# The attention mask written into the score banks by ScalarE instead of added by TensorE

## The chip, the cores and the metric

One core of a Trainium2 chip runs the whole program in one launch. The metric is the device time of that core in microseconds (us); lower is better. All times here come from three timed runs of the kernel before and from one profiled execution of it.

## The reference, cut to what matters

The program is a model of 13 phases over 256 tokens (272 with 16 meta tokens in the first half): eight feed-forward networks, two "hybrid mixers" with stick-breaking attention beside a 31-tap convolution, one differential attention, one retention, and one norm. The change touches the two mixers. Their attention is:

```python
z = jnp.einsum('bhqd,bhkd->bhqk', qb, kh) * scale
valid = key_pos < qpos
log_keep = jnp.where(valid, jax.nn.log_sigmoid(-z), 0.0)
after = lax.cumsum(log_keep, axis=3, reverse=True) - log_keep
attn = jnp.where(valid, jnp.exp(jax.nn.log_sigmoid(z) + after), 0.0)
return jnp.einsum('bhqk,bhkd->bhqd', attn, vh)
```

There are 8 heads of 64 dimensions. Only keys before the query count; the others are masked by adding -1e30 to z. The feed-forward networks, `(silu(x @ w_gate) * (x @ w_up)) @ w_down`, matter here because their buffers move in memory.

## The kernel before, in words

All matrices are float32. Every weight panel (128 x 1024 or 128 x 1408) is loaded by SyncE's queue into `raw`, split by ScalarE into a rounded part `whi` (L432) and by VectorE into the rest `wlo` (L439), and used once: TensorE forms three products per tile, x_hi by whi (L416), x_lo by whi (L423) and x_hi by wlo (L424). The ring of panels has four slots. Each matmul has its own weight load (PEld in the profile), which overlaps the matmul before it.

**Order of the work.** There is no scheduler: each engine's list is written out by hand, and waits on semaphores join them. In a mixer TensorE runs panels 0 to 16, and then four groups p = 0 to 3, one per pair of heads. A group is: `scores(p)` (18 small matmuls L720 into banks 6 and 7, and two matmuls L727 that add the mask, identity by `mask_r`, to columns 0:144 and 288:432 of each bank), a panel, `weighted_values(2p-1)` (L770), a panel, `suffix_sums(2p)` (L751 to L756), a panel, `suffix_sums(2p+1)` and `weighted_values(2p)`, a panel. In group 3 a matmul L795 with `mean_512` stands behind `suffix_sums(6)`; it waits for `ysum_step`, the sum over the convolution's channels that GpSimd makes (L2153, L2158) when its taps (L2149) are through.

ScalarE's list in a group: `log_terms` of both heads (L1262 to L1266, behind `z_full`), `terms_hi` (L1273), two panels' splits, `weights_hi(2p)` (L1279 and L1282, exponentials of the bank), four tap products for GpSimd (L1217), a panel's split, `weights_hi(2p+1)`, `out_hi(2p)` (L1287), up to four tap products, a panel's split. `weights_hi` is the last reader of its bank before the next pair's scores, which wait for it through `at_hi_ready`.

**Where the buffers lie.** The program's buffers stand in each partition one behind the other, in the order of their declaration, each rounded up to 32 bytes. `raw`, `whi`, `wlo`, `h` and `u` come before `consts`; `hid` (the input of the feed-forwards' second product), `qk`, `ao_hi`, `ao_lo`, `ry`, `dy_hi`, `rqk_hi` and others come behind it. `consts` has 10 x 128 floats (5120 bytes). From the sizes follows the offset of the moving operand x of a matmul against the weight tile that is loaded while it runs, in bytes modulo 256:

| operands | matmuls | offset before |
|---|---|---|
| u by whi, wlo | all gate, up and mixer input panels | 192 |
| hid by whi, wlo | 8 feed-forwards, second product: 2640 of 256 columns, 1584 of 272 | 192 |
| ry by whi, wlo | output of the retention: 384 of 256 columns | 192 |
| dy_hi, dy_lo by dw | three panels of the differential attention | 64 |
| qk, ao by whi, wlo | tail of the mixers | 192, 192, and 128 for the third of each three (x and weights both advance by 64 bytes per tile, so the next tile's weights are 64 nearer) |
| rqk_hi, rqk_lo by each other | retention scores | 0 |

For hid: 22528 (whi) + 22528 (wlo) + 8704 (h) + 20480 (u) + 3 x 1088 + 32 + 5120 (consts) + 3712 (constants and gains) + 96 (the place in `hid`) = 86464 = 337 x 256 + 192.

Of the kernel before, what the change touches and what calls it, by code (L numbers as in the profile page):

```python
# [12 lines left out]
T = META + SEQ  # L13
# [149 lines left out]
def build(nc, w8, w11, xT, small, cst, lam, outT):  # L163
# [7 lines left out]
    with ctx:  # L171
        def sb(name, shape, dt=f32, where=None):
            return (where or ctx).enter_context(nc.sbuf_tensor(name, shape, dt))

        def sem(name):
            return ctx.enter_context(nc.semaphore(name))
# [14 lines left out]

        consts = sb("consts", [128, CONSTS, 128])
        mean_d, mean_512, mean_128, mean_64, ident, ones_f, tri_f = (consts[:, i, :] for i in range(7))
        masks = consts[:, :, :].rearrange("p a c -> p (a c)")[:, 7 * 128:7 * 128 + 2 * MASKED]
        ones_r = sb("ones_r", [128, 128], f32r)
        tri_r = sb("tri_r", [128, 128], f32r)
        ident_r = sb("ident_r", [128, 128], f32r)
# [83 lines left out]
        with ExitStack() as area:  # L283
# [60 lines left out]

        qk_hi_ready, qk_ready, vt_full, v_hi_ready, v_ready = (
            sem(s) for s in ("qk_hi_ready", "qk_ready", "vt_full", "v_hi_ready", "v_ready"))
        z_full, az_done, e_done, l_done, nlk_done = (
            sem(s) for s in ("z_full", "az_done", "e_done", "l_done", "nlk_done"))
        lk_hi_ready, lk_ready, c_full = (sem(s) for s in ("lk_hi_ready", "lk_ready", "c_full"))
# [284 lines left out]
        def _(pe):  # L634
# [55 lines left out]
            def mix(y, l):  # L690
# [15 lines left out]
                def scores(p):  # L706


                    pe.wait_ge(qk_ready, 8 * l + 2 * p + 2)
                    if p == 0:  # L710
                        pe.wait_ge(const_r, 5 + l)
                        pe.wait_ge(v_ready, 3 * l + 2)
                    if PAIRS * l + p > 0:
                        pe.wait_ge(at_hi_ready, SB_HEADS * l + 2 * p)
                    for i, (s0, c0, w) in enumerate(S_TILES):
                        for n, (kt, qt) in enumerate(((0, 8), (0, 12), (4, 8))):
                            ks, qs = (kt + p) * T + KEY_AT[i], (qt + p) * T + s0
                            for m in range(2):
                                rows = slice(64 * m, 64 * m + 64)
                                pe.matmul(bank[6 + m][:, c0:c0 + w], flat[rows, ks:ks + 128], flat[rows, qs:qs + w],  # L720
                                          start=(i == 0 and n == 0), stop=False, skip_group_check=True)


                    for m in range(2):
                        whole = bank[6 + m][:, :]
                        two = bass.AP(whole.tensor, whole.offset, [whole.ap[0], [SECOND, 2], [1, MASKED]])
                        pe.matmul(two, ident_r[:, :], mask_r[:, :].rearrange("p (a c) -> p a c", c=MASKED), start=False,  # L727
                                  stop=True, skip_group_check=True).then_inc(z_full, 1)
# [403 lines left out]
        def _(act):  # L1132
# [66 lines left out]
            def mix(y, l):  # L1199
# [75 lines left out]
                def weights_hi(hd):  # L1275
                    act.wait_ge(c_full, H + hd + 1)
                    if hd >= 1:
                        act.wait_ge(at_ready, H + hd)
                    act.activation(ex[:, :], bank[6 + hd % 2][:, 0:SW], ACT.Exp)  # L1279
                    if hd >= 2:  # L1280
                        act.wait_ge(o_full, H + hd - 1)
                    act.activation(at_hi[:, hd % 2, :], bank[6 + hd % 2][:, 0:SW], ACT.Exp).then_inc(at_hi_ready, 1)  # L1282

                def out_hi(hd):
                    rows = slice(64 * (hd % 2), 64 * (hd % 2) + 64)
                    act.wait_ge(o_full, H + hd + 1)
                    act.activation(ao_hi[rows, hd // 2, :], bank[5][rows, 0:T], ACT.Copy).then_inc(ao_hi_ready, 1)  # L1287

                for p in range(PAIRS):
                    j, n = FIRST_PANELS + 4 * p, POOL_HEAD_TAPS[p]  # L1290
                    log_terms(2 * p)
                    tap_products(n[0])
                    log_terms(2 * p + 1)
                    terms_hi(2 * p)
                    panel(j)
                    terms_hi(2 * p + 1)
                    if p > 0:
                        out_hi(2 * p - 1)
                    panel(j + 1)
                    weights_hi(2 * p)  # L1300
                    tap_products(n[1])
                    if p == PAIRS - 1:
                        for c in range(CH):
                            act.wait_ge(yc_done, CH * l + c + 1)
                            act.activation(cpad[:, c, CPAD:CPAD + N2], proj[:, A_SLOT + c, W2], ACT.Square)\
                               .then_inc(ysq_done, 1)
                    panel(j + 2)
                    if p == PAIRS - 1:
                        weights_hi(2 * p + 1)
                        out_hi(2 * p)  # L1310
                    if p < PAIRS - 1:
                        weights_hi(2 * p + 1)
                        out_hi(2 * p)
                    tap_products(n[2])
                    panel(j + 3)
                j = FIRST_PANELS + 4 * PAIRS
# [260 lines left out]
        def _(dve):  # L1577
# [95 lines left out]
            def mix(y, l):  # L1673
# [33 lines left out]
                if l == 0:  # L1707
# [6 lines left out]
                    dve.tensor_copy(tri_r[:, :], tri_f).then_inc(const_r, 1)  # L1714
                    dve.tensor_copy(ident_r[:, :], ident).then_inc(const_r, 1)
                    dve.tensor_copy(mean_64r[:, :], mean_64).then_inc(const_r, 1)
                dve.tensor_copy(mask_r[:, :], masks).then_inc(const_r, 1)
                def qk_lo(i):
                    hi, lo = (i // 2, 4 + i // 2) if i % 2 else (8 + i // 2, 12 + i // 2)
                    dve.wait_ge(qk_hi_ready, 8 * l + i + 1)  # L1720
# [389 lines left out]
        @block.gpsimd  # L2110
        def _(pool):
            pool_update(pool, 0)
            pool.dma_start(consts[:, 1:CONSTS, :], cst[:, 128:CONSTS * 128].rearrange("p (a c) -> p a c", c=128))\
                .then_inc(const_loaded, 16)
            pool.dma_start(sgain[:, :], small[:, GAINS:GAINS + SMALLS]).then_inc(const_loaded, 16)
            pool.dma_start(lam_in[:, :, :], lam.partition_broadcast(128)).then_inc(const_loaded, 16)
# [1 line left out]
            for y, kind in enumerate(PHASES):  # L2118
                if kind in ("da", "rt"):

                    pool.wait_ge(panel_used, BASE[y]["P"])
                    at = {"da": CONSTS * 128, "rt": CONSTS * 128 + 384}[kind]
                    dst = {"da": dist, "rt": rdist}[kind]
                    pool.dma_start(dst[:, :], cst[:, at:at + 384]).then_inc(table_loaded, 16)
                if kind == "da":
# [54 lines left out]
GAINS = len(PHASES) * KD  # L2180
SMALLS = 2 * CH * (CONV_K + 3) + 3 + 16
CONST_LOADS = 3
CONSTS = 10


def tables():

    p = np.arange(128)[:, None]
    c = np.arange(128)[None, :]
    one = np.ones((128, 128))  # L2190
    parts = [one / D, one / 512, one / 128, (p // 64 == c // 64) / 64.0, p == c, -one, -1.0 * (p >= c)]
    far = 1e30
    last = np.where((p >= 128 - (T - 256)) & (c > p - (128 - (T - 256))), 0.0, -far)[:, 0:T - 256]
    seen = np.zeros((128, 3 * 128 - 2 * MASKED + T - 256))
    parts += [last, np.where(c > p, 0.0, -far), np.where(c > p, 0.0, -far), seen]
    for d in (p - c, 128 + p - np.arange(256)[None, :],
              np.arange(256)[None, :] - p, c - p):
        parts.append(np.where(d >= 0, d, far))
    return np.ascontiguousarray(np.concatenate([np.asarray(x, np.float64) for x in parts], 1), np.float32)
# [79 lines left out]
```

## Time and profile before

| | us |
|---|---|
| median of 3 runs (2171.69 to 2171.99) | 2171.73 |
| the profiled execution's own time | 2172.23 |
| its span | 2170.4 |
| TensorE matmuls busy | 2159.0 (99%) |
| VectorE busy | 1473.0 (68%) |
| ScalarE busy | 1202.2 (55%) |
| GpSimd busy | 283.9 (13%) |

The mean granted TensorE clock of the execution is 1.000, that is 2.4 GHz. A matmul's duration in a row is its latency through a pipeline: consecutive matmuls start much closer together (some 0.12 us) than they last (some 0.28 us). What a stream costs is read from the distance of the starts.

### The profile page before, as it was taken

The page shows a single profiled execution, that of the slowest core. Times are in us where ns is not written, and L with a number is a line of the kernel's source. Part 1 is how long each engine was busy: PE and PEld are TensorE (multiplying, and loading weights), DVE is VectorE, ACT ScalarE, POOL GpSimd, SP SyncE. Part 2 cuts the span into 40 slices and gives each one's busy share as a digit, 9 for nine tenths or more (in the row PEclk, how much of TensorE's full clock was granted, in tenths as well). Part 3 has the DMA queues.
Part 4 walks back from the last instruction along what each step waited for, and adds up shares of the span by engine and source line. Part 5 has one row for each costly group of instructions (what it writes and reads, how often), then busy time and mean ns, then how long its engine had stood idle before and what let it go on. Part 6 is the DMA issues. An engine that isn't in the chain of part 4 may idle for free.

```text
span 2170.4 us, 48317 instructions
## 1 busy us (share of the span) xinstructions
PE 2159.0 (99%) x18139; PEld 2141.7 (99%) x18139; DVE 1473.0 (68%) x2242; ACT 1202.2 (55%) x1752; POOL 283.9 (13%) x328
## 2 busy tenths in 40 slices
PE   8999999999999999999999999999999999999999
PEld 8999999999999999999999999999999999999999
DVE  6655998665566579876657657976656745686663
ACT  6444786544444368755555546865445535565552
POOL 0001661100100136220020011010010010101000
PEclk9999999999999999999999999999999999999999
DMA  6555435556455554455656655356656655445664
GB/s 233 176 192 167 163 118 175 175 174 198 153 181 186 182 165 142 149 177 193 205 180 194 200 188 170 117 184 191 207 173 195 209 178 180 161 158 195 193 217 131
DMA packets 100401, 386.57 MB, mean 178 GB/s; under 512 B 11312, under 2 KB 12464, under 8 KB 100304
## 3 DMA queue, kind: packets, MB, share of 16 engines
q1 hardware_dynamic: 99648, 383.89, 53.7%
q0 software_dynamic: 368, 1.26, 0.2%
q8 instruction: 62, 1.02, 0.2%
q14 instruction: 35, 0.29, 0.0%
q10 hardware_dynamic: 288, 0.12, 0.0%
HBM read 384.18 MB, written 1.05 MB: 177 GB/s over the span
## 4 chain that ended last, share of the span: by engine, by line
PE 91%; DVE 6%; ACT 2%; issue 1%; DMA 0%; SPq 0%; ACTq 0%; DVEq 0%
PE bank L423 28%; PE bank L416 28%; PE bank L424 28%; DVE wlo L439 2%; DVE bank L1702 1%; PE bank L1056 1%; PE bank L1058 1%; PE bank L1057 1%; ACT whi L432 1%; PE bank L1103 0%; PE bank L770 0%; DVE proj L1688 0%; PE bank L947 0%; PE bank L950 0%; PE bank L949 0%
## 5 line engine op out<-in xcount | busy, mean ns | idle before, releaser
L416 PE MATMUL bank<-u,whi 128*128 128x256 f32 (+2 forms) x3776 | 1062.6, 281 | 7.3 <-DVE u L477 7.3
L423 PE MATMUL bank<-u,whi 128*128 128x256 f32 (+1 forms) x3776 | 1062.1, 281 | 0.0
L424 PE MATMUL bank<-u,wlo 128*128 128x256 f32 (+1 forms) x3776 | 1060.0, 281 | 0.0
L439 DVE TENSOR_TENSOR wlo<-raw,whi 128x1024 fp32r<-128x1024 f32 (+1 forms) x677 | 892.7, 1321 | 186.1 <-ACT whi L432 185.5
L432 ACT ACTIVATE whi<-raw 128x1024 fp32r<-128x1024 f32 (+1 forms) x677 | 743.5, 1112 | 192.3 <-PE bank L424 172.0
L416 PEld LDWEIGHTS bank<-u,whi 128*128 128x128 f32 x3776 | 711.3, 188 | 8.5 <-DVE wlo L439 7.2
L423 PEld LDWEIGHTS bank<-u,whi 128*128 128x128 f32 x3776 | 711.3, 188 | 0.9 <-issue 0.2
L424 PEld LDWEIGHTS bank<-u,wlo 128*128 128x128 f32 x3776 | 711.1, 188 | 0.0
L416 PE MATMUL bank<-hid,whi 128*128 128x256 f32 (+1 forms) x1408 | 394.2, 280 | 0.0
L423 PE MATMUL bank<-hid,whi 128*128 128x256 f32 (+1 forms) x1408 | 394.2, 280 | 0.0
L424 PE MATMUL bank<-hid,wlo 128*128 128x256 f32 (+1 forms) x1408 | 394.2, 280 | 0.0
L1639 DVE TENSOR_TENSOR up<-bank,R 128x256 f32<-128x256 f32 (+1 forms) x176 | 75.8, 431 | 289.5 <-PE bank L424 289.5
L416 PEld LDWEIGHTS bank<-hid,whi 128*128 128x128 f32 x1408 | 264.6, 188 | 0.0
L424 PEld LDWEIGHTS bank<-hid,wlo 128*128 128x128 f32 x1408 | 264.6, 188 | 0.0
L423 PEld LDWEIGHTS bank<-hid,whi 128*128 128x128 f32 x1408 | 264.6, 188 | 0.0
L464 ACT ACTIVATE u<-h,gain 128x256 fp32r<-128x256 f32 (+1 forms) x88 | 44.2, 512 | 268.3 <-DVE h L1604 262.5
L1174 ACT ACTIVATE sl<-gt 128x256 f32<-128x256 f32 (+1 forms) x160 | 67.7, 423 | 198.0 <-DVE gt L1637 198.0
L1179 ACT ACTIVATE hid<-pr 128x256 f32 (+2 forms) x160 | 67.8, 424 | 152.9 <-DVE pr L1644 152.9
L1604 DVE SCALAR_TENSOR_TENSOR h<-bank,h 128x256 f32<-128x256 f32 (+1 forms) x88 | 37.9, 430 | 163.9 <-PE bank L424 163.8
L513 POOL TENSOR_TENSOR ssq<-h 128x256 f32<-128x256 f32 (+1 forms) x10 | 6.2, 624 | 1029.0 <-DVE h L1604 1029.0
L2149 POOL TENSOR_TENSOR proj<-proj,tprod 128x272 f32<-128x272 f32 (+1 forms) x120 | 121.7, 1034 | 54.6 <-ACT tprod L1217 49.8
L518 POOL TENSOR_TENSOR sq<-h 128x256 f32<-128x256 f32 (+1 forms) x70 | 45.0, 644 | 345.9 <-DVE h L1604 344.9
(297 smaller groups left out, 2190.8 us busy)
## 6 DMA issues: line engine op xcount, KB each, us to landing
raw<-w SPq DMA_DIRECT2D x552, 512.0 KB, 3.3
raw<-w SPq DMA_DIRECT2D x128, 704.0 KB, 4.8
h<-xT SPq DMA_DIRECT2D x4, 272.0 KB, 5.6
outT<-h SPq DMA_DIRECT2D x8, 128.0 KB, 5.0
consts<-cst POOLq DMA_DIRECT2D x1, 576.0 KB, 5.0
dist<-cst POOLq DMA_DIRECT2D x1, 192.0 KB, 2.8
rdist<-cst POOLq DMA_DIRECT2D x1, 192.0 KB, 3.7
sgain<-small POOLq DMA_DIRECT2D x1, 145.5 KB, 5.4
```

What stands on the lines that cost most here:

```text
L416: pe.matmul(out[:, cut:cols], w, x[:, cut:cols], start=first, stop=False, skip_group_check=True)
L423: pe.matmul(out, w_h, x_lo, start=False, stop=False, skip_group_check=True)
L424: return pe.matmul(out, w_l, x_hi, start=False, stop=last, skip_group_check=True)
L432: act.activation(weights(0, n), raw[:, n % RING, 0:COLS[n]].rearrange("p (k c) -> p k c", c=128), ACT.Copy).then_inc(hi_ready, 1)
L439: dve.tensor_tensor(weights(1, n), raw[:, n % RING, 0:COLS[n]].rearrange("p (k c) -> p k c", c=128), weights(0, n), ALU.subtract).then_inc ...
L464: act.activation(u_at(y, 0, f), h[:, f, win(y)], ACT.Copy, scale=norm_gain(y, f)).then_inc(u_hi_ready, 1)
L518: pool.tensor_tensor(sq[:, win(y)], h[:, f, win(y)], h[:, f, win(y)], ALU.mult).then_inc(sq_done, 1)
L1174: act.activation(sl[:, p, W], gt[:, p, W], ACT.Silu).then_inc(silu_done, 1)
L1179: act.activation(hid_at(y, 0, f), pr[:, p, W], ACT.Copy).then_inc(hid_hi_ready, 1)
L1604: dve.scalar_tensor_tensor(out=h[:, f, W], in0=src, scalar=factor, in1=h[:, f, W], op0=ALU.mult, op1=ALU.add).then_inc(h_done, 1)
L1639: dve.tensor_tensor(up[:, p, W], bank[(g + 1) % 4][:, 0:N], R[:, W], ALU.mult).then_inc(a_evac, 1)
L2149: pool.tensor_tensor(acc, acc, tprod[:, m % TAP_RING, W2], ALU.add)\
```

## The change

ScalarE's new step `masked(hd)` copies the mask of all 432 score columns from `consts` (float32, the middle 144 columns zero) into bank 6 or 7. It stands behind `weights_hi(2p)` for head 2p+2 and behind `out_hi(2p)` for head 2p+3, for p = 0 to 2. The scores of pairs 1 to 3 then start no new sum (start is set only at p = 0), so that they are added to what lies in the bank; they wait for the new semaphore `z_masked`, and their last matmul on each bank gives `z_full`. The two mask matmuls stay for pair 0 of each mixer. `consts` becomes 7 x 128 + 432 = 1328 floats in place of 1280, one flat row, loaded by the same DMA in one piece per partition; `mask_r` is cast from its first and third 144 columns.

```diff
-        consts = sb("consts", [128, CONSTS, 128])
-        mean_d, mean_512, mean_128, mean_64, ident, ones_f, tri_f = (consts[:, i, :] for i in range(7))
-        masks = consts[:, :, :].rearrange("p a c -> p (a c)")[:, 7 * 128:7 * 128 + 2 * MASKED]
+        consts = sb("consts", [128, CONSTS])
+        mean_d, mean_512, mean_128, mean_64, ident, ones_f, tri_f = (consts[:, 128 * i:128 * i + 128] for i in range(7))
+
+        mask = consts[:, CONSTS - SW:CONSTS]
+        masks = mask.rearrange("p (a c) -> p a c", c=MASKED)[:, 0:3:2, :]
...
+                    if p > 0:
+                        pe.wait_ge(z_masked, (SB_HEADS - 2) * l + 2 * p)
...
-                                pe.matmul(bank[6 + m][:, c0:c0 + w], flat[rows, ks:ks + 128], flat[rows, qs:qs + w],
-                                          start=(i == 0 and n == 0), stop=False, skip_group_check=True)
-
-
-                    for m in range(2):
+                                mm = pe.matmul(bank[6 + m][:, c0:c0 + w], flat[rows, ks:ks + 128], flat[rows, qs:qs + w],
+                                               start=(p == 0 and i == 0 and n == 0), stop=False, skip_group_check=True)
+                                if p > 0 and i == 2 and n == 2:
+                                    mm.then_inc(z_full, 1)
+
+                    for m in range(2 if p == 0 else 0):
...
+                def masked(hd):
+
+                    act.wait_ge(at_hi_ready, H + hd - 1)
+                    act.activation(bank[6 + hd % 2][:, 0:SW], mask, ACT.Copy).then_inc(z_masked, 1)
+
...
                     weights_hi(2 * p)
+                    if p < PAIRS - 1:
+                        masked(2 * p + 2)
                     tap_products(n[1])
...
                         weights_hi(2 * p + 1)
                         out_hi(2 * p)
+                        masked(2 * p + 3)
                     tap_products(n[2])
...
-CONSTS = 10
+CONSTS = 7 * 128 + SW
```

**What moves in memory.** Everything behind `consts` lies 192 bytes further on; `whi`, `wlo` and `u` stay. The offsets of the table become: hid and ry by whi and wlo 128 (86464 + 192 = 338 x 256 + 128), qk and ao 128, 128 and 64; u stays at 192; pairs that both lie behind `consts` (dy by dw, rqk by rqk) keep theirs.

**What moves on the engines.** TensorE in the second mixer at the scores of pair 2, in the program before (`qk` are the scores, `u` by `whi` the next panel):

```order
L424 MATMUL bank<-u,wlo 128x256
L720 MATMUL bank<-qk 128x272 [waits at_hi_ready,qk_ready]
L720 MATMUL bank<-qk 128x272 x5
L720 MATMUL bank<-qk 128x144 x6
L720 MATMUL bank<-qk 128x16 x6
L727 MATMUL bank<-mask_r,ident_r 128x2x144 x2
L416 MATMUL bank<-u,whi 128x256 [waits a_evac,lo_ready]
```

The same place in the changed program (L725 is the score's line there, L419, L426 and L427 the products'):

```order
L427 MATMUL bank<-u,wlo 128x256
L725 MATMUL bank<-qk 128x272 [waits z_masked,at_hi_ready,qk_ready]
L725 MATMUL bank<-qk 128x272 x5
L725 MATMUL bank<-qk 128x144 x6
L725 MATMUL bank<-qk 128x16 x6
L419 MATMUL bank<-u,whi 128x256 [waits a_evac,lo_ready]
```

The two mask matmuls are gone in three groups of each mixer, and the first score has one more wait.

ScalarE in the second mixer, second half of group 2, before:

```order
L1279 ACTIVATE ex<-bank 128x432 [waits at_ready,c_full]
L1282 ACTIVATE at_hi<-bank 128x432 [waits o_full]
L1217 ACTIVATE tprod<-cpad,sgain 128x256 [waits pool_tap_done] x4
L432 ACTIVATE whi<-raw 128x1024 [waits panel_used,raw_loaded3]
L1279 ACTIVATE ex<-bank 128x432 [waits at_ready,c_full]
L1282 ACTIVATE at_hi<-bank 128x432 [waits o_full]
L1287 ACTIVATE ao_hi<-bank 64x272 [waits o_full]
L1217 ACTIVATE tprod<-cpad,sgain 128x256 [waits pool_tap_done] x4
```

And in the changed program (L1293 is the new copy):

```order
L1285 ACTIVATE ex<-bank 128x432 [waits at_ready,c_full]
L1288 ACTIVATE at_hi<-bank 128x432 [waits o_full]
L1293 ACTIVATE bank<-consts 128x432 [waits at_hi_ready]
L1223 ACTIVATE tprod<-cpad,sgain 128x256 [waits pool_tap_done] x4
L435 ACTIVATE whi<-raw 128x1024 [waits panel_used,raw_loaded3]
L1285 ACTIVATE ex<-bank 128x432 [waits at_ready,c_full]
L1288 ACTIVATE at_hi<-bank 128x432 [waits o_full]
L1298 ACTIVATE ao_hi<-bank 64x272 [waits o_full]
L1293 ACTIVATE bank<-consts 128x432 [waits at_hi_ready]
L1223 ACTIVATE tprod<-cpad,sgain 128x256 [waits pool_tap_done] x4
```

Both copies stand ahead of tap products for GpSimd; the second has only these between it and the next panel's split.

## Rows read from the trace of the kernel before

**Rows 1.** The page, busy time of the engines
```profile
PE 2159.0 (99%) x18139; PEld 2141.7 (99%) x18139; DVE 1473.0 (68%) x2242; ACT 1202.2 (55%) x1752; POOL 283.9 (13%) x328
```

**Rows 2.** The page, the chain that ended last, by engine
```profile
PE 91%; DVE 6%; ACT 2%; issue 1%; DMA 0%; SPq 0%; ACTq 0%; DVEq 0%
```

**Rows 3.** Waits of TensorE: for whom, us in total, times, longest
```profile
PE bank L416 <- DVE u L477: 7.3, 1, 7.3
```

**Rows 4.** Timeline of TensorE, first mixer: start us, us
```profile
275.73 0.52 PE L727 MATMUL bank<-mask_r,ident_r 128*128 128x288 f32 x2
276.09 0.29 PE L416 MATMUL bank<-u,whi 128*128 128x272 f32 x1
276.22 0.28 PE L423 MATMUL bank<-u,whi 128*128 128x272 f32 x1
...
280.02 0.37 PE L416 MATMUL bank<-u,whi 128*128 128x272 f32 x1
280.23 0.29 PE L423 MATMUL bank<-u,whi 128*128 128x272 f32 x1
```

**Rows 5.** ScalarE's operation of 432 columns from SBUF to SBUF: busy us, mean ns
```profile
L1273 ACT ACTIVATE lk_hi<-proj 128x432 fp32r<-128x432 f32 x16 | 8.9, 556 | 1.8 <-DVE proj L1752 1.8
```

**Rows 6.** Timeline of ScalarE and TensorE, end of group 0, first mixer
```profile
272.44 0.39 ACT L1287 ACTIVATE ao_hi<-bank 64x272 fp32r<-64x272 f32 x1
274.58 1.22 PE L720 MATMUL bank<-qk 64*128 64x272 f32 x18
```

**Rows 7.** Timeline of ScalarE, second mixer, group 2
```profile
871.41 0.53 ACT L1282 ACTIVATE at_hi<-bank 128x432 fp32r<-128x432 f32 x1
871.82 1.70 ACT L1217 ACTIVATE tprod<-cpad,sgain 128x256 f32<-128x256 f32 x4
```

**Rows 8.** Timeline of GpSimd, then TensorE, first mixer, then second mixer
```profile
315.25 2.08 POOL L2158 TENSOR_TENSOR sq<-sq,proj 128x272 f32<-128x272 f32 x2
...
318.61 0.48 PE L795 MATMUL bank<-sq,consts 128*128 128x272 f32 x1
...
872.41 10.96 POOL L2149 TENSOR_TENSOR proj<-proj,tprod 128x256 f32<-128x256 f32 x9 [4.90 <-ACT tprod L1217]
884.33 2.08 POOL L2158 TENSOR_TENSOR sq<-sq,proj 128x256 f32<-128x256 f32 x2
...
886.71 0.46 PE L795 MATMUL bank<-sq,consts 128*128 128x256 f32 x1
```

**Rows 9.** Timeline of TensorE, a feed-forward's second product, then the second mixer's tail
```profile
1099.92 0.28 PE L424 MATMUL bank<-hid,wlo 128*128 128x256 f32 x1
...
1101.39 0.28 PE L416 MATMUL bank<-hid,whi 128*128 128x256 f32 x1
...
934.80 0.28 PE L423 MATMUL bank<-qk,whi 128*128 128x256 f32 x1
...
936.34 0.28 PE L424 MATMUL bank<-qk,wlo 128*128 128x256 f32 x1
```

**Rows 10.** TensorE's matmuls by operands and shape: count, busy us, mean ns
```profile
L423 PE MATMUL bank<-hid,whi 128*128 128x256 f32 x880 | 242.9, 276 | 0.0
L423 PE MATMUL bank<-hid,whi 128*128 128x272 f32 x528 | 151.3, 286 | 0.0
L423 PE MATMUL bank<-ry,whi 128*128 128x256 f32 x128 | 35.3, 276 | 0.0
L1036 PE MATMUL bank<-dy_hi,dw_hi 128*128 128x256 f32 x24 | 6.6, 276 | 0.0
L424 PE MATMUL bank<-qk,wlo 128*128 128x256 f32 x96 | 27.1, 283 | 0.0
L416 PE MATMUL bank<-qk,whi 128*128 128x272 f32 x96 | 27.7, 289 | 0.0
L423 PE MATMUL bank<-qk,whi 128*128 128x272 f32 x96 | 27.4, 285 | 0.0
L1089 PE MATMUL bank<-rqk_lo,rqk_hi 128*128 128x256 f32 x8 | 2.2, 280 | 0.0
```

More of the change, by code:

```diff
@@ L346, in build @@
             sem(s) for s in ("qk_hi_ready", "qk_ready", "vt_full", "v_hi_ready", "v_ready"))
+        z_masked = sem("z_masked")
         z_full, az_done, e_done, l_done, nlk_done = (
@@ L1716, in mix @@
                     dve.tensor_copy(mean_64r[:, :], mean_64).then_inc(const_r, 1)
-                dve.tensor_copy(mask_r[:, :], masks).then_inc(const_r, 1)
+                dve.tensor_copy(mask_r[:, :].rearrange("p (a c) -> p a c", c=MASKED), masks).then_inc(const_r, 1)
                 def qk_lo(i):
@@ L2112, in _ @@
             pool_update(pool, 0)
-            pool.dma_start(consts[:, 1:CONSTS, :], cst[:, 128:CONSTS * 128].rearrange("p (a c) -> p a c", c=128))\
+            pool.dma_start(consts[:, 128:CONSTS], cst[:, 128:CONSTS])\
                 .then_inc(const_loaded, 16)
@@ L2121, in _ @@
                     pool.wait_ge(panel_used, BASE[y]["P"])
-                    at = {"da": CONSTS * 128, "rt": CONSTS * 128 + 384}[kind]
+                    at = {"da": CONSTS, "rt": CONSTS + 384}[kind]
                     dst = {"da": dist, "rt": rdist}[kind]
@@ L2193, in tables @@
     last = np.where((p >= 128 - (T - 256)) & (c > p - (128 - (T - 256))), 0.0, -far)[:, 0:T - 256]
-    seen = np.zeros((128, 3 * 128 - 2 * MASKED + T - 256))
-    parts += [last, np.where(c > p, 0.0, -far), np.where(c > p, 0.0, -far), seen]
+    parts += [last, np.where(c > p, 0.0, -far), np.zeros((128, MASKED)), np.where(c > p, 0.0, -far),
+              np.zeros((128, T - 256))]
     for d in (p - c, 128 + p - np.arange(256)[None, :],
```

## The prediction

> **What bounds the kernel now.** I read the page's busy times first: TensorE's matmuls are busy for 2159.0 of 2170.4 us [rows 1]. The chain that ended last then shows that this is the bound, not merely activity: 91% of it is TensorE [rows 2], and the longest of TensorE's waits in total is 7.3 us, a single one at the start of the program [rows 3]. So the time is the number of matmuls times the distance of their starts. An edit pays if it removes matmuls or shortens that distance, and costs if it lengthens it; what ScalarE, VectorE or GpSimd do counts only where they make TensorE wait. The timeline gives the distances and the grouping by shape the durations, which serve as a second gauge: a longer distance shows in both.
>
> The sum is made against the profiled execution, 2172.23 us (2170.4 of span and 1.8 around it). The median of the runs is 2171.73, 0.5 less, and I take 0.5 off at the end.
>
> **Part 1: the mask matmuls that go.** Six groups lose a pair of L727. From the first of the pair to the panel's first L416 it is 276.09 - 275.73 = 0.36 us [rows 4]. Not all of it comes back. Behind the pair, L416 follows L423 at 276.22 - 276.09 = 0.13; where L416 stands directly behind a small matmul, the same step takes 280.23 - 280.02 = 0.21 [rows 4], and that is where it will stand now. So a group gives 0.36 - 0.08 = 0.28 us, and six give -1.7. Bounds: nothing of the step is lost, 6 x 0.36 = -2.2; the whole 0.21 is new, 6 x 0.15 = -0.9.
>
> **Part 2: ScalarE's twelve copies.** No row shows ScalarE writing 432 columns from SBUF into a bank. From SBUF to SBUF such an operation takes 0.56 us [rows 5], from a bank 0.53 [rows 7]; I take 0.53. The nearest other rows of one pass over a tile bound it, 0.38 (L1287, 272 columns [rows 6]) and 0.56; the second rival has a higher price. The copies are 6.4 us of ScalarE, which is busy 55%; the question is who waits.
>
> (a) The scores wait for `z_masked`. The tightest place is group 0 of the first mixer: `out_hi` ends at 272.44 + 0.39 = 272.83 and the scores start at 274.58 [rows 6], 1.75 us later. The first copy delays everything behind it by about 0.57: 0.41 of issue distance plus the 0.12 for which the copy must wait until its own predecessor has ended (871.41 + 0.53 against the 871.82 at which the next operation starts now [rows 7]), and a little for the semaphore. The second adds 0.53. That is 1.1 of 1.75; 0.65 is left, so I cost it at nothing. Queued behind the copies are tap products and the split of a panel that TensorE needs only three panels later (24 matmuls of 0.12 each, almost 9 us), so the split's delay is hidden too.
>
> (b) The tap products feed GpSimd. In group 2 of the second mixer GpSimd starts nine adds right behind the delayed product, at 872.41, runs them back to back, and ends its sums at 884.33 + 2.08 = 886.41; TensorE's L795, which waits for them, starts at 886.71 [rows 8]. The slack is 0.30 us. TensorE will be there 3 x 0.28 = 0.84 earlier. GpSimd's start moves by +0.57 (the copy) and -0.56 (two groups shortened ahead of it), so not at all. TensorE then waits 0.84 - 0.30 = 0.5 us. Bounds: 0 (if the product comes as early as TensorE does) and +1.1 (the full 0.57 on top). In the first mixer the same slack is 318.61 - (315.25 + 2.08) = 1.28 us [rows 8], more than 0.84, and I take nothing.
>
> **Part 3: the 192 bytes.** This edit is not about the mask, and it is the largest term. `consts` grows by 48 floats, so `hid` and `ry` move against `whi` and `wlo`: their offset goes from 192 to 128 modulo 256, at every one of their matmuls. The rows show two speeds for one and the same shape of 256 columns. In the stream of `hid`, 13 steps take 1101.39 - 1099.92 = 1.47 us, 113 ns each; in the mixer's tail 13 steps take 936.34 - 934.80 = 1.54, 118.5 each [rows 9]. The durations say the same: 276 ns for hid and ry (offset 192) and dy by dw (64), 283 for the matmul of qk that meets 128, and 280 for rqk, at 0 [rows 10]. The pattern that fits is that a weight load and a moving operand whose addresses differ by a multiple of 128 disturb each other. It is a reading of few rows, and qk and rqk differ from hid in more than this.
>
> The price: between ends far apart, nothing and the 7 ns of qk by wlo (283 against 276), I take the row in which every step lies on a multiple of 128, as it will in hid: rqk, 280 against 276, 4 ns. 3 x 880 of hid and 3 x 128 of ry are 3024 matmuls x 4 = 12.1 us. For 272 columns the difference is smaller: 289 and 285 for qk, in the middle 287, against 286 for hid, 1 ns x 1584 (3 x 528) = 1.6 [rows 10]. Together +13.7. Bounds: 0, and 3024 x 7 + 1584 x 3 = 25.9. Below nothing: no row of 256 columns is faster than 276, whatever its offset, so I leave only a small chance for a gain. qk and ao go from one multiple of 128 in three to two in three; their speed is off already, and I take 0.
>
> A rule of the Trainium skill speaks against this term. TensorE: Matmul & The Clock Gate, section "Step-by-step: what each phase is for", says that the array has two independent read ports, and that loading the next weights does not take bandwidth from the running matmul. By it part 3 would be 0 and the time that of the first rival below; the trace agrees as far as loads overlap matmuls everywhere, but it does not explain two speeds for one shape.
>
> **The rest.** The cast of the mask reads the same number of columns, the load of `consts` is one DMA at the start, needed only in the first mixer: 0.
>
> **Sum.** 2172.23 - 1.7 + 0.5 + 13.7 = 2184.7; less 0.5 for the median, 2184.2, say 2184.
>
> **Rivals.**
> First, not slower: addresses do not matter and only the queues count. The offset's term is 0, and -1.7 + 0.5 = -1.2 on the median gives 2170.5. For it: hid has no row at 128, and qk's slower step could come from its other layout (tiles 1088 bytes apart). Against it: rqk, of another layout, is slow too, and rows at 64 and 192 are alike. The mechanism decides at 0 ns per step; up to 1.8 ns (5.5 us over 3024) the time would still be called the same.
>
> Second, the wait moves to ScalarE: the copy into a bank takes twice what I take, 1.1 us, so that both copies delay `out_hi`'s successor by 2.2 and the scores wait some 0.5 us in each of six groups. Without the address term that is -1.2 + 3.0 = +1.8, 2173.5. Rows 5 and 7 speak against it: operations of 432 columns take 0.53 to 0.56.
>
> Third, the change does more than it says in the good direction: at 128 the load and the operand interleave better than at 192, for example 3 ns per matmul, 3024 x 3 = -9, with the -1.2 giving 2161.5. No row supports it.
>
> **How the numbers follow.** Forecast (address term between 1.8 and 8 ns) 0.59; first rival 0.33; second 0.03; third 0.05. About 0.2% (4.3 us) is what a measurement of this kernel can tell from no change. Slower by more: 0.59. Within: 0.33 + 0.03 = 0.36. Faster: 0.05. The range must take in the first rival: it goes from 2169.5 (part 1 at its bound of -2.2 and no wait in 2b) to 2194 (the address term at 23.5, near its upper end). The forecast's own range is 2178 to 2194.
>
> **What would show it.** hid and ry by whi and wlo of 256 columns at 280 ns or more, with starts 117 to 120 ns apart, while u stays at 276 and 113: part 3 right. If they stay at 276, the step of part 3 has failed, and the time is near 2170.5. Twelve rows of the copy at 0.5 to 0.56 us and no wait of the scores on them: part 2a right. A wait of L795 on GpSimd of about 0.5 us in the second mixer: part 2b right. Scores followed by L416 and L423 at a distance of 0.21 us: part 1 right. If u too changes speed, the cause is not the offset that I name.

## The result and the profile after

| | before | after |
|---|---|---|
| median of 5 runs each, same chip, us | 2171.99 (2171.69 to 2172.32) | 2194.85 (2194.60 to 2198.95) |
| profiled execution and its span, us | 2172.23, 2170.4 | 2194.60, 2192.8 |

By the medians the changed kernel is slower by 22.9 us. Over all runs it takes 1.0111 of the time before, interval 1.0101 to 1.0122; two of its five runs lie some 4 us above the other three. The forecast was slower by 12, with 2194 as the end of its range. The direction is right; the largest term was put at 13.7 us and measured 21.6.

The page's busy times and its chain by engine, in the changed kernel [rows 1, 2]:

```profile
PE 2180.7 (99%) x18127; PEld 2163.4 (99%) x18127; DVE 1470.8 (67%) x2242; ACT 1206.6 (55%) x1764; POOL 283.5 (13%) x328
...
PE 92%; DVE 3%; issue 2%; ACT 2%; POOL 1%; DMA 0%; POOLq 0%; ACTq 0%; DVEq 0%
```

There are 12 matmuls fewer (18127 against 18139), and TensorE is busy for 21.7 us more. The span grew by 22.4. TensorE's waits are no place for that [rows 3]; the columns are the total in us, how often, and the longest:

```profile
PE bank L419 <- DVE u L480: 7.3, 1, 7.3
PE bank L801 <- POOL sq L2172: 0.8, 1, 0.8
PE bank L744 <- DVE proj L1702: 0.4, 1, 0.4
PE bank L757 <- DVE lk_lo L1773: 0.4, 1, 0.4
```

The first is the start of the program, as before. The second and the fourth are new and small: the sums' matmul L801 waits for GpSimd, and a suffix sum L757 for `lk_lo`. A wait of 0.2 on VectorE at the tail of the second mixer is new too, and stands in the kernel with the 192 bytes alone as well. The scores (L725) do not appear.

Which matmuls slowed is read from the grouping by operands and shape [rows 5, 10], count, busy us, mean ns:

```profile
L426 PE MATMUL bank<-u,whi 128*128 128x256 f32 x2272 | 630.5, 278 | 0.0
L419 PE MATMUL bank<-hid,whi 128*128 128x256 f32 x880 | 247.7, 281 | 0.0
L419 PE MATMUL bank<-hid,whi 128*128 128x272 f32 x528 | 153.0, 290 | 0.0
L426 PE MATMUL bank<-ry,whi 128*128 128x256 f32 x128 | 36.3, 284 | 0.0
L427 PE MATMUL bank<-qk,wlo 128*128 128x256 f32 x96 | 26.7, 278 | 0.0
L1293 ACT ACTIVATE bank<-consts 128x432 f32<-128x432 f32 x12 | 6.3, 529 | 0.2
```

`hid` went from 276 to 281 ns and from 286 to 290; `ry` from 276 to 284; `u`, whose place did not change, is at 278 (277 before). The starts say how much of that is time. A feed-forward's second product after [rows 9], start and duration in us; 13 steps lie between the two rows, and 1.54 us, 118.5 ns each where it was 113:

```profile
1109.92 0.28 PE L427 MATMUL bank<-hid,wlo 128*128 128x256 f32 x1
...
1111.46 0.28 PE L419 MATMUL bank<-hid,whi 128*128 128x256 f32 x1
```

Over a whole stretch, from the first start of a second product to its last, the traces give the following (each stretch of hid has 527 steps, that of ry 383):

| stretch | count | before, us | after, us | difference in all |
|---|---|---|---|---|
| hid, 256 columns | 5 | 59.73 | 62.54 | +14.1 |
| hid, 272 columns | 3 | 65.00 | 66.75 | +5.3 |
| ry, 256 columns | 1 | 43.75 | 46.00 | +2.3 |

That is 21.6 of the span's 22.4. From the last second product ahead of it to the first panel of the next feed-forward, the first mixer is 0.16 us longer than before (its tail's matmuls of `qk`, 272 columns, take 0.22 more) and the second 0.81 shorter. So some 1.4 us lie elsewhere. The largest part is in the retention: it has five short stretches of u by `whi` and `wlo`, and four of them run at 118 ns a step where it was one before, which makes 0.95 us in all. The offset of u is 192 in both kernels. By shape, 1819.5 to 1826 us in the kernel before, then 1835.5 to 1842 in the changed one:

```profile
L424 PE MATMUL bank<-u,wlo 128*128 128x256 f32 x20 | 5.5, 276 | 0.0
...
L427 PE MATMUL bank<-u,wlo 128*128 128x256 f32 x20 | 5.6, 281 | 0.0
```

The experiments come back to such a change of speed without a change of offset.

The removed matmuls, in group 0 of the first mixer after [rows 4, 6]; `x18` are the scores in one row:

```profile
275.78 1.21 PE L725 MATMUL bank<-qk 64*128 64x272 f32 x18
276.92 0.39 PE L419 MATMUL bank<-u,whi 128*128 128x272 f32 x1
277.15 0.28 PE L426 MATMUL bank<-u,whi 128*128 128x272 f32 x1
277.27 0.29 PE L427 MATMUL bank<-u,wlo 128*128 128x272 f32 x1
```

L426 follows L419 at 0.23 us, where 0.21 was foreseen. From the first score to the third product it is 277.27 - 275.78 = 1.49 us; over the six groups the mean of that distance fell from 1.75 to 1.49, which is 0.26 per group and 1.6 us in all. ScalarE at the same place:

```profile
274.24 0.38 ACT L1298 ACTIVATE ao_hi<-bank 64x272 fp32r<-64x272 f32 x1
274.52 0.52 ACT L1293 ACTIVATE bank<-consts 128x432 f32<-128x432 f32 x1
```

The copy ends at 275.04, and the scores that need it start at 275.78: a slack of 0.74 us, where 0.65 was foreseen. In the second mixer GpSimd, then TensorE [rows 8]:

```profile
877.43 10.43 POOL L2163 TENSOR_TENSOR proj<-proj,tprod 128x256 f32<-128x256 f32 x9 [5.09 <-ACT tprod L1223]
...
888.82 2.84 POOL L2172 TENSOR_TENSOR sq<-sq,proj 128x256 f32<-128x256 f32 x2
...
891.71 0.70 PE L801 MATMUL bank<-sq,consts 128*128 128x256 f32 x2 [0.77 <-POOL sq L2172]
```

The nine adds moved with the program and take 10.43 us, where they took 10.96. The two sums behind them take 2.84 us, where they took 2.08; L801 waits 0.77 for them. One by one, with what VectorE does beside them, the sums are, first in the kernel before, then in the changed one:

```profile
884.33 0.75 POOL L2158 TENSOR_TENSOR sq<-sq,proj 128x256 f32<-128x256 f32 x1
885.20 0.60 DVE L1759 TENSOR_TENSOR lk_lo<-proj,lk_hi 128x432 fp32r<-128x432 f32 x1
885.22 1.19 POOL L2158 TENSOR_TENSOR sq<-sq,proj 128x256 f32<-128x256 f32 x1
```

```profile
888.79 0.60 DVE L1773 TENSOR_TENSOR lk_lo<-proj,lk_hi 128x432 fp32r<-128x432 f32 x1
888.82 1.17 POOL L2172 TENSOR_TENSOR sq<-sq,proj 128x256 f32<-128x256 f32 x1
889.64 1.43 DVE L442 TENSOR_TENSOR wlo<-raw,whi 128x1024 fp32r<-128x1024 f32 x1
890.13 1.52 POOL L2172 TENSOR_TENSOR sq<-sq,proj 128x256 f32<-128x256 f32 x1
```

A sum takes 1.17 to 1.19 us beside `lk_lo`, 1.52 beside the rest of a split into `wlo`, and 0.75 where neither runs. In the kernel before one of the two sums met such an operation of VectorE, in the changed one both did.

### The profile page after: what moved, and what is told of

Its sections match the earlier page's. It is cut to its first block, busy times and chain, and to the rows that moved or that the text cites. A ratio compares the mean times of both kernels' runs of the same rounds, so it can differ in the third digit from the quotient of the medians.

```text
span 2192.8 us, 48305 instructions
## 1 busy us (share of the span) xinstructions
PE 2180.7 (99%) x18127; PEld 2163.4 (99%) x18127; DVE 1470.8 (67%) x2242; ACT 1206.6 (55%) x1764; POOL 283.5 (13%) x328
## 4 chain that ended last, share of the span: by engine, by line
PE 92%; DVE 3%; issue 2%; ACT 2%; POOL 1%; DMA 0%; POOLq 0%; ACTq 0%; DVEq 0%
PE bank L426 28%; PE bank L419 28%; PE bank L427 28%; DVE wlo L442 1%; POOL proj L2163 1%; DVE bank L1716 1%; PE bank L1062 1%; PE bank L1064 1%; PE bank L1063 1%; ACT whi L435 1%; PE bank L889 1%; PE bank L1109 0%; PE bank L776 0%; PE bank L953 0%; PE bank L955 0%
## 5 line engine op out<-in xcount | busy, mean ns | idle before, releaser
L419 PE MATMUL bank<-u,whi 128*128 128x256 f32 (+2 forms) x3776 | 1063.4, 282 | 7.3 <-DVE u L480 7.3
L426 PE MATMUL bank<-u,whi 128*128 128x256 f32 (+1 forms) x3776 | 1062.2, 281 | 0.0
L427 PE MATMUL bank<-u,wlo 128*128 128x256 f32 (+1 forms) x3776 | 1060.2, 281 | 0.0
L419 PEld LDWEIGHTS bank<-u,whi 128*128 128x128 f32 x3776 | 711.3, 188 | 8.8 <-DVE wlo L442 7.5
L426 PEld LDWEIGHTS bank<-u,whi 128*128 128x128 f32 x3776 | 710.9, 188 | 0.9 <-issue 0.2
L427 PEld LDWEIGHTS bank<-u,wlo 128*128 128x128 f32 x3776 | 710.8, 188 | 0.0
L419 PE MATMUL bank<-hid,whi 128*128 128x256 f32 (+1 forms) x1408 | 400.6, 285 | 0.0
L427 PE MATMUL bank<-hid,wlo 128*128 128x256 f32 (+1 forms) x1408 | 400.6, 285 | 0.0
L426 PE MATMUL bank<-hid,whi 128*128 128x256 f32 (+1 forms) x1408 | 400.6, 285 | 0.0
L427 PEld LDWEIGHTS bank<-hid,wlo 128*128 128x128 f32 x1408 | 265.1, 188 | 0.0
L419 PEld LDWEIGHTS bank<-hid,whi 128*128 128x128 f32 x1408 | 265.1, 188 | 0.0
L426 PEld LDWEIGHTS bank<-hid,whi 128*128 128x128 f32 x1408 | 265.1, 188 | 0.0
```

The source lines that it names most:

```text
L419: pe.matmul(out[:, cut:cols], w, x[:, cut:cols], start=first, stop=False, skip_group_check=True)
L426: pe.matmul(out, w_h, x_lo, start=False, stop=False, skip_group_check=True)
L427: return pe.matmul(out, w_l, x_hi, start=False, stop=last, skip_group_check=True)
```

## The experiments

Each kernel is the one before or the changed one with the lines shown. "Stretch" is the distance from first to last start as in the table above; the offsets are of the moving operand against `whi` and `wlo`, modulo 256 bytes.

**Is it the 192 bytes, or the mask?** `e2_shift_only` is the kernel before with the bytes alone; `e1_mask_realigned` is the changed kernel with 64 bytes more, so that everything behind `consts` lies 256 bytes further on than before and all offsets are the old ones.

```diff
e2_shift_only, against before
         consts = sb("consts", [128, CONSTS, 128])
...
+        sb("consts_pad", [128, 48])
e1_mask_realigned, against after
         consts = sb("consts", [128, CONSTS])
...
+        sb("consts_pad", [128, 16])
```

> The kernel before, with 48 unused floats behind consts: the change's 192 bytes without its mask part. Address theory: hid 281 and 290 ns, ry 282 to 285, as in the change, and a time of 2172.0 + 22.9 + 0.8 = 2195.7, somewhat above the change. Rival (the rhythm comes from the mask part): the time of before, 2172, and hid at 276.

> The change, with 16 floats (64 bytes) left free behind consts, so that everything behind it lies 256 bytes further on than before and all offsets against whi and wlo are those of before. Address theory: hid by whi of 256 columns back at 276 ns and 113 ns apart (after: 281 and 118.7), of 272 columns at 286 (after: 290), ry at 276; the loss of some 22 us is gone and only the mask part is left, -1.6 for six shorter groups and +0.8 for L801's wait on GpSimd: about 2171.2, 0.8 below before. Rival (the mask matmuls that are gone let TensorE's stream enter another rhythm, which it keeps in the feed-forwards): hid stays at 281 and the time near 2194.

`e2_shift_only`: 2194.76 us (2194.44 to 2195.05), ratio 1.0105 (1.0089 to 1.0120). The 192 bytes alone, without any copy, give the whole loss. `e1_mask_realigned`: median 2176.66 of 11 runs (2171.16 to 2177.77), ratio 1.0013 (1.0004 to 1.0022). The ratio takes in all runs, whose means are 2174.9 and 2172.0: the whole change with the old offsets is slower by 0.13%, and its runs are spread wider than those of the kernel before (the last experiments). By operands and shape, first `e2_shift_only`, then `e1_mask_realigned`:

```profile
L424 PE MATMUL bank<-hid,whi 128*128 128x256 f32 x880 | 247.6, 281 | 0.0
L424 PE MATMUL bank<-hid,whi 128*128 128x272 f32 x528 | 153.0, 290 | 0.0
L424 PE MATMUL bank<-ry,whi 128*128 128x256 f32 x128 | 36.0, 281 | 0.0
```

```profile
L427 PE MATMUL bank<-hid,whi 128*128 128x256 f32 x880 | 242.9, 276 | 0.0
L427 PE MATMUL bank<-hid,whi 128*128 128x272 f32 x528 | 151.3, 286 | 0.0
L427 PE MATMUL bank<-ry,whi 128*128 128x256 f32 x128 | 35.9, 280 | 0.0
```

hid follows the offset exactly, with stretches of 62.54 and 66.75 us in the one and 59.73 and 65.00 in the other. ry does not: it is slow in `e1_mask_realigned` (280 ns, 45.25 us) though its offset is 192 again. That, and the two heaps in which the runs of this kernel lie, is a thing of its own, taken up last.

**Which offsets are bad?** The place of `hid` is set for each feed-forward by a table, in floats, so one execution tries eight places on the kernel before. Apart from 128 and 192, each offset rests on one product of a shape, in one execution.

```diff
-HID_PLACE = {0: (24, 0), 2: (24, 0), 3: (24, 0), 5: (24, 0), 7: (24, 0), 9: (24, 0), 10: (24, 0), 12: (24, 0)}
+HID_PLACE = {0: (40, 0), 2: (56, 0), 3: (8, 0), 5: (8, 0), 7: (40, 0), 9: (56, 0), 10: (16, 0), 12: (32, 0)}   # e3_hid_places
+HID_PLACE = {0: (16, 0), 2: (88, 0), 3: (32, 0), 5: (88, 0), 7: (48, 0), 9: (28, 0), 10: (20, 0), 12: (0, 0)}  # e5_hid_places_2
```

> The kernel before, with the place of hid changed feed-forward by feed-forward, nothing else. Offsets modulo 256 of hid against whi and wlo, in the order of the eight second products: 0, 64, 128 (272 columns), then 128, 0, 64, 160, 224 (256 columns). Theory 'multiples of 128 are bad': 64 as fast as 192 (64.9 us a product of 272 columns from the first to the last start, 59.6 of 256), 0 and 128 alike at 66.6 and 62.4; at 160 and 224, half way, anything between. Rival 'only 192 is good': 64 as slow as 128. Rival 'only the absolute address of hid counts, or what others write': the slow products don't follow this order.

> A second map of places of hid in the kernel before. Offsets modulo 256 in the order of the eight second products: 160, 192 (but 256 bytes further on), 224 for 272 columns; then 192 (256 bytes further on), 32, 208, 176, 96 for 256 columns. In the first map only 192 was fast (65.0 and 59.7 us a product), and 0, 64, 128, 160 and 224 cost 1.1 to 3.5 us. Theory 'the offset modulo 256 decides, and only near 192 is good': both products at 192 + 256 fast, 32 and 96 slow (61.8 to 63.2), and 176 and 208 show how wide the good place is. Rival 'the absolute place decides': 192 + 256 is slow too.

One run each: 2190.15 and 2186.43 us. A place of 24 floats is offset 192; each float more adds 4 bytes, so 88 floats are 256 bytes more and 192 again. The stretches in us:

| offset | 0 | 32 | 64 | 96 | 128 | 160 | 176 | 192 | 192, 256 bytes on | 208 | 224 |
|---|---|---|---|---|---|---|---|---|---|---|---|
| 256 columns | 63.22 | 61.49 | 62.07 | 63.23 | 62.54 | 61.84 | 62.85 | 59.73 | 59.73 | 62.80 | 62.35 |
| 272 columns | 66.05 | | 66.75 | | 66.75 | 65.01 | | 65.00 | 65.00 | | 66.05 |

Rows by shape of single feed-forwards. `e3_hid_places` at 0, then at 64:

```profile
L423 PE MATMUL bank<-hid,whi 128*128 128x256 f32 x176 | 49.8, 283 | 0.0
...
L424 PE MATMUL bank<-hid,wlo 128*128 128x256 f32 x176 | 49.1, 279 | 0.0
```

and `e5_hid_places_2` at 192 and 256 bytes on, then at 32:

```profile
L423 PE MATMUL bank<-hid,whi 128*128 128x256 f32 x176 | 48.6, 276 | 0.0
...
L423 PE MATMUL bank<-hid,whi 128*128 128x256 f32 x176 | 49.2, 279 | 0.0
```

The reading "multiples of 128 disturb" falls: 32, 96, 160, 176, 208 and 224 are slow too. Of the ten offsets tried with 256 columns only 192 ran fast, and it comes again 256 bytes further on; for 272 columns 160 is as good. The place of before was the good one, and the change left it.

For 64 this is not shown. Its stretch of 62.07 us goes in steps of 117 to 119 ns, 117.8 in the mean. At 128 they are uneven, 115 to 122, while 117 to 119 with the same mean, and the same 62.07 us, is what hid at 192 does in the second rhythm found below. So the product at 64 may have been in that rhythm, and no second run of it was made.

**Is it where hid lies, or where it lies against the weights?** `e6_all_shifted` moves everything from `whi` on by 64 bytes, so that no offset changes; `e7_u_too` moves everything behind `wlo` by 192, so that u is at 128 as well; `e8_wlo_only` puts `whi` at the good offset and `wlo` at 128, one load in three.

```diff
e6_all_shifted, behind the declaration of raw
+        sb("w_pad", [128, 16])
e7_u_too, behind the declaration of wlo
+        sb("w_pad", [128, 48])
e8_wlo_only, behind whi and behind wlo
+        sb("w_pad", [128, 16])
...
+        sb("x_pad", [128, 48])
```

> The kernel before with 16 unused floats between raw and whi: all weights and all moving operands lie 64 bytes further on, and no offset between them changes. Offset theory: 2171.8, all products as before. Rival (absolute addresses decide): hid, ry and perhaps u slow, 20 us or more.

> The kernel before with 48 unused floats between wlo and h: u moves by 192 bytes against whi and wlo too, to offset 128, beside hid, ry, qk and ao. Offset theory: what hid lost in e2 (5.35 ns a step at 256 columns, 3.3 at 272) is lost by u as well: 6788 x 5.35 + 4500 x 3.3 = 51 us on top of 23, about 2246. Rival (something of hid and ry alone, for example who writes them while they are read): 2195 as e2.

> The kernel before with 16 unused floats between whi and wlo and 48 between wlo and h: the offset of every moving operand to whi is 192 as before, that to wlo 128. One weight load in three has the bad offset. If each load pays for itself, hid loses a third of what it lost in e2: 59.73 + 0.9 = 60.7 us a product, and all of the kernel about a third of e7's 74: 2196. If one bad load in three keeps the stream in the slow rhythm (as in qk before, 118.4 ns a step with one in three at 128), nearly all is lost: 62.3 a product, some 2240.

`e6_all_shifted`: 2172.03 us (2171.61 to 2173.91), ratio 0.9998 (0.9987 to 1.0009), every stretch as before. So the absolute place does not matter for a shift of 64 bytes of all of them. `e7_u_too`: 2241.03 (2240.93 to 2241.14), ratio 1.0315 (1.0285 to 1.0345). Its matmuls of u:

```profile
L424 PE MATMUL bank<-u,whi 128*128 128x256 f32 x2272 | 641.3, 282 | 0.0
...
L424 PE MATMUL bank<-u,whi 128*128 128x272 f32 x1504 | 436.8, 290 | 0.0
```

A feed-forward's first product goes from 120.35 to 125.84 us (256 columns) and from 130.58 to 134.09 (272). It is not a thing of hid: u, when it leaves the good offset, loses 5.3 ns in 256 columns and 3.3 in 272, as hid did. The total is 5 us below the 2246 expected. `e8_wlo_only`: one run, 2235.83. Its u by `whi`, then by `wlo`:

```profile
L425 PE MATMUL bank<-u,whi 128*128 128x256 f32 x2272 | 641.7, 282 | 0.0
L426 PE MATMUL bank<-u,wlo 128*128 128x256 f32 x2272 | 635.1, 280 | 0.0
```

One bad load in three costs nearly as much as three: u's stretches are 125.38 and 134.05 us. This fits qk in the tail, which was slow before (118.5 ns [rows 9]) with one load in three at 128. With two of three its 256 columns did not become slower (119.4 to 119.0 ns a step), its 272 columns a little (124.4 to 125.1).

A rival that these runs leave is that not the load disturbs the matmul but the writing of the next panels into `whi` and `wlo` by ScalarE and VectorE, whose places move with them. The trace of the changed kernel answers it: of the 527 steps of the first stretch of hid with 256 columns, 300 start while one of the two writes a panel and 227 while neither does, and both kinds are 118.7 ns long; 124 steps with ScalarE, VectorE and GpSimd all idle are 118.7 as well.

**What is the mask worth by itself?** In `e1_mask_realigned` the first mixer is 0.20 us shorter than before and the second 0.31, and the waits are those of the changed kernel (1.0 on GpSimd, 0.4 on `lk_lo`). In its other two traces, `e9_e1_again` and `e10_e1_third` below, the two together are 0.43 and 0.54 shorter. `e4_copy_behind_taps` puts the first copy behind the tap products; `e11_copy_by_mixer` does so in the first mixer alone.

```diff
e4_copy_behind_taps, against e1_mask_realigned
                     weights_hi(2 * p)
+                    tap_products(n[1])
                     if p < PAIRS - 1:
                         masked(2 * p + 2)
-                    tap_products(n[1])
e11_copy_by_mixer, against e1_mask_realigned
-                    if p < PAIRS - 1:
+                    if p < PAIRS - 1 and l == 1:
                         masked(2 * p + 2)
                     tap_products(n[1])
+                    if p < PAIRS - 1 and l == 0:
+                        masked(2 * p + 2)
```

> e1 with the first copy, masked(2p+2), behind the tap products in place of ahead of them, so that GpSimd's products are not delayed. If the wait of L801 on GpSimd (0.8 us in the change) comes from this copy's 0.57 us: it falls to about 0.2 to 0.3, and the time is 0.5 below e1, some 2170.7. Rival (the wait is due to TensorE's coming 0.8 earlier alone): no difference from e1.

> e1 with the first copy behind the tap products in the first mixer (as e4, where that mixer was 0.58 us shorter than before against 0.20 in e1) and ahead of them in the second (as e1, 0.31 shorter against 0.56 longer in e4). If the two mixers are independent: 0.6 + 0.3 = 0.9 below before, near 2170.9, where the run keeps its fast rhythm. Rival: the gain is less than what the rhythm of ry and u varies by from run to run (1.5 to 6 us), and the comparison says no difference.

`e4_copy_behind_taps`: 2172.15 (2171.39 to 2174.17), ratio 1.0001 (0.9992 to 1.0010). Its waits of TensorE:

```profile
PE bank L758 <- DVE lk_lo L1774: 1.4, 3, 0.9
```

The wait on GpSimd is gone, and three on `lk_lo` have taken its place: the first mixer is 0.55 us shorter than before, the second 0.55 longer. `e11_copy_by_mixer` takes the better order for each, and its mixers are 0.59 and 0.28 shorter; its runs lie at 2170.57 to 2178.97, median 2176.38, ratio 1.0011 (1.0002 to 1.0020). So the most that the mask gave in the traces is 0.9 us, and no version beat the kernel before.

**Why two heaps?** Of 11 runs of `e1_mask_realigned` four lie below 2171.8 and six above 2176.6; of 11 of `e11_copy_by_mixer` seven lie above 2176.3. None of the 45 runs of before beside the experiments is above 2174, nor any of the 11 of `e4_copy_behind_taps` above 2174.2. The kernel `e1_mask_realigned` was profiled twice more.

> e1 once more, for its trace: its 11 runs lay at 2171.2 to 2171.7, at 2173.7 and at 2176.7 to 2177.8. If whole stretches fall into a slow rhythm although all offsets are 192, a run near 2177 shows one or two stretches of u or ry with 281 ns in place of 276 and starts 117 to 118 ns apart; ry did so in the run of 2173.7 (45.3 us in place of 43.8). If the 6 us are waits, they stand in the waits of TensorE.

> The same kernel again, to have both kinds of run on trace: one near 2171.5 and one near 2177, or the same twice.

They came out at 2171.99 and 2177.15 us. In the second one a single feed-forward is longer: first product 124.38 against 120.87 us, second 62.07 against 59.73, 5.85 in all, with every offset at 192. TensorE in `e10_e1_third` where it begins, start and duration:

```profile
1163.86 0.28 PE L427 MATMUL bank<-u,whi 128*128 128x256 f32 x1
1163.97 0.28 PE L428 MATMUL bank<-u,wlo 128*128 128x256 f32 x1
1164.11 0.38 PE L420 MATMUL bank<-u,whi 128*128 128x256 f32 x1
1164.33 0.28 PE L427 MATMUL bank<-u,whi 128*128 128x256 f32 x1
```

and its wait there:

```profile
PE bank L420 <- DVE wlo L443: 0.2, 1, 0.2
```

The steps were 113.3 ns up to here. From the short wait at 1164.11 on they are 117.8, and stay so until 1317. The profile puts the wait down to `wlo`, but that operation was over at 1163.74:

```profile
1162.51 1.23 DVE L443 TENSOR_TENSOR wlo<-raw,whi 128x1024 fp32r<-128x1024 f32 x1 [1.10 <-ACT whi L436]
```

So it is not shown what TensorE waited for. By shape, in 1150 to 1250 us, `e10_e1_third` and then `e9_e1_again`:

```profile
L420 PE MATMUL bank<-u,whi 128*128 128x256 f32 x285 | 80.0, 281 | 0.0
```

```profile
L420 PE MATMUL bank<-u,whi 128*128 128x256 f32 x295 | 81.5, 276 | 0.0
```

So there are two rhythms at one and the same offset, and an execution can fall from the fast into the slow one and keep it for 150 us. The profile of `e11_copy_by_mixer`, a run of 2176.89, shows the same flip at the same place. A hitch alone does not decide it: `e9_e1_again` has a step of 0.22 us from 1164.81 to 1165.03 and goes on at 113.3. ry shows the same (43.75 us in before and 43.77 in `e4_copy_behind_taps`, 45.25 in `e1_mask_realigned` and `e5_hid_places_2`, all at 192), and so do the short stretches of u in the retention, one of which was slow in the kernel before too.

All six traces of a program with the copies have a hitch of some 0.2 us at this place of the program, and the traces of before, `e2_shift_only`, `e3_hid_places`, `e5_hid_places_2` and `e6_all_shifted`, without copies, have none. So as far as these runs show, the upper heap comes with the mask's program and not with an offset, though not in every order of it, as `e4_copy_behind_taps` shows. With it `e1_mask_realigned` is 2.9 us above before in the mean, where its lower runs are at or below it. Why the hitch is there, and what decides whether the rhythm flips, stays open.

## Why the prediction was right in direction and too small

**Part 1, the mask matmuls, foreseen -1.7: right.** Measured 6 x 0.26 = -1.6, with the step behind the scores at 0.23 us instead of 0.21. (The working has two names the wrong way round: it is L423 that follows L416.)

**Part 2a, scores and copies, foreseen 0: right for the scores,** with 0.74 us of slack at the tightest place and copies of 0.53 us. But a suffix sum in the first mixer waits 0.4 for `lk_lo`, and that wait was no term of the sum. The larger part of it is no delay at all: the `lk_lo` that it waits for ends 8.57 us behind the score at 274.58 [rows 6] in the kernel before and 8.70 behind that at 275.78 in the changed one, and TensorE comes to it 0.27 earlier. With the first copy moved away (`e4_copy_behind_taps`) it ends at 8.56 and TensorE still waits 0.2. What was missed is that VectorE had no slack there.

**Part 2b, GpSimd, foreseen +0.5: mechanism right, size 0.8** (1.0 in `e1_mask_realigned`), within its bounds. I had GpSimd at its old durations. The nine adds take 0.53 us less and the two sums 0.76 more, so 0.23 more in all, because other operations of VectorE fall beside them; and GpSimd starts some 0.2 later against the program, where nothing was foreseen. In the first mixer there is no such wait, as foreseen. A wait of 0.4 on `at_lo` that the kernel before had is gone. The saving of 1.6, less 1.0 and 0.4 and plus that 0.4, is 0.6; the mixers of `e1_mask_realigned` show 0.5.

**Part 3, the 192 bytes, foreseen +13.7: this step failed in its size, and its rule was wrong.** The cause is right: `e2_shift_only` has the loss without the change, `e1_mask_realigned` has hid's speed back. The size is hid's +14.1 for 256 columns and +5.3 for 272, and ry's +2.3, 21.6 in all. In the terms of the working, a matmul of 256 columns costs 5.3 ns of distance and not 4, one of 272 costs 3.3 and not 1. I took both from other operands' rows: the 4 ns from rqk, and the 1 ns from qk, whose 272 columns are 1 ns above hid in durations [rows 10] and 1.0 in distances (124.4 ns against 123.3). hid itself lost 5 and 4 ns in durations, so duration was a fair gauge; the rows that stood in for hid were not. The distances that the same section had at hand, 118.5 against 113 [rows 9], give 5.5 x 3024 = 16.6, within 0.3 of the 16.3 that hid and ry of 256 columns measured. Of ry's share up to 1.5 us may be the rhythm, since it has that at 192 as well.

**The end of the range.** With 21.6 in place of 13.7 the sum would have been 2192, inside the range. The measured median lies above 2194 because the rest went the same way: the mixers are 0.65 us shorter and not 1.2, and 1.4 us lie in stretches that had no term, u's in the retention above all. The working's own bound for the address term was 25.9, and the range was closed at 23.5.

**The reading behind it,** that multiples of 128 disturb, was drawn from three kinds of rows and is wrong: of ten offsets only 192 ran fast for 256 columns. It gave the right sign because the change left 192, and there it was lucky: by that reading offsets 160 and 224 would have been free, and they measured 61.84 and 62.35 us in place of 59.73. dy by dw, at 64, runs at 276 ns [rows 10]; as said above, the table does not show that 64 is slow.

**The rule weighed against it.** The Trainium skill, "TensorE: Matmul & The Clock Gate", section "Step-by-step: what each phase is for", would have the next weight load take no read bandwidth from the running matmul. By that the term would be 0, and for these matmuls it is not: with the same instructions, the offset between loaded and moving tile alone changes the step from 113.3 to 118.7 ns. What collides inside the chip, and whether it is read bandwidth that is lost, no run here shows.

**The rivals.** The first, addresses do not matter, falls with `e2_shift_only`. The second, a slow copy, falls with twelve copies at 529 ns. The third, a gain at 128, is excluded by hid's rows. One sign of being wrong asked whether u changes speed: its long stretches do not (114.1 us each, before and after), its short ones in the retention do. They point to the second rhythm as something beside the offset, which the prediction did not have.

## What to carry to other kernels

A change of a buffer's size is a change of the placement of all buffers behind it; where TensorE is the bound, pad it back to a multiple of 256 bytes, or compare against a kernel with the padding alone, before anything else is concluded of the change. Price a stream by the distance of its starts in a stream of the same shape and rhythm, not by the duration of another operand's rows. Where matmuls are removed, list everything that TensorE will now reach earlier and ask what slack it has, not only what the new instructions delay: here waits on GpSimd and VectorE left 0.5 of 1.6 us. And compare the spread of the runs, not only their median: two orders of the same work had a second heap 5 us up, and a third had none.

## What the runs showed of the hardware

- The offset between the moving operand and the weight tile that is loaded beside it, modulo 256 bytes, changes the step of such matmuls: 113.3 ns at 192 against 116.7 (32) to 120.0 (0 and 96) for 256 columns, 123.3 (192 and 160) against 125.3 to 126.7 for 272. Moved together, they lose nothing (`e6_all_shifted`). Only 128 was measured many times, and 64 may be the rhythm of the third point.
- One load of three at a bad offset costs nearly what three cost (u's stretch 125.38 against 125.84 us, from 120.35).
- At the good offset there is a second rhythm of 117.8 ns, which an execution can fall into at a hitch of 0.2 us and keep for 150 us; it made 5.85 us of difference between two executions of one kernel. It stands in short stretches of the kernel before too.
- GpSimd's add of 128 x 256 floats takes 1.17 to 1.52 us beside VectorE's `lk_lo` and `wlo`, and 0.75 where neither of them runs.
- ScalarE writes 128 x 432 floats from SBUF into a bank in 0.53 us, against 0.56 from SBUF to SBUF [rows 5] and 0.53 from a bank to SBUF [rows 7].
